# Moving one layer's table building behind the gate on the vector engine, in a one-core hybrid S5 / gated DeltaNet backbone

## The reference

```python
def swiglu(h, w13, w2):
    a, b = jnp.split(h @ w13, 2, axis=-1)
    return (jax.nn.silu(a) * b) @ w2
x = x + 0.5 * gate * swiglu(ada_norm(x, g, shift, scale), w13, w2)
...
abar = exp(dt * (a_re + i a_im))          # S5: 64 groups of 16 channels, 64 complex states each
h_t = abar * h_{t-1} + f * (B u_t)        # as an associative scan, in both directions
y_t = Re(C h_t)
```

## Time and profile before

| what | value |
|---|---|
| time, median of 3 runs | 2175.92 us (2172.47 to 2176.16) |
| profiled execution's own time | 2172.47 us |
| its span, first to last instruction | 2170.7 us |
| mean granted TensorE clock | 0.948 |
| PE / DVE / ACT / POOL busy | 1984.7 / 1476.4 / 698.9 / 589.1 us |

### The profile page before, as it was taken

How to read it: one execution, slowest core, us unless ns; L and a number is a source line. 1 busy time by engine, 2 the same in 40 slices (tenths; PEclk the granted TensorE clock), 3 DMA queues, 4 the chain that set the end, 5 groups by cost and what they waited for, 6 DMA issues and landing times.

```text
span 2170.7 us, 37461 instructions
## 1 busy us (share of the span) xinstructions
PE 1984.7 (91%) x14700; PEld 1684.0 (78%) x14700; DVE 1476.4 (68%) x2265; ACT 698.9 (32%) x1110; POOL 589.1 (27%) x473
## 2 busy tenths in 40 slices
PE   3999999991889899999979999998999999989997
PEld 0778778771788678888858888886888889879997
DVE  8958778764434596784889668346677777746555
ACT  2322222222123322221234222123555555426332
POOL 2254774752442231120233112023000000022113
PEclk9999999995759899999999999999999999889999
DMA  8364565549952354444535444222211111114553
GB/s 318 141 239 166 204 212 184 200 161 205 293 159 97 116 187 162 154 169 141 187 103 184 156 154 171 95 80 80 74 41 41 41 50 50 41 59 139 184 181 97
DMA packets 104736, 310.20 MB, mean 143 GB/s; under 512 B 27680, under 2 KB 39456, under 8 KB 95136
## 3 DMA queue, kind: packets, MB, share of 16 engines
q1 hardware_dynamic: 89392, 285.67, 39.6%
q10 hardware_dynamic: 12528, 12.33, 1.8%
q0 software_dynamic: 2688, 10.42, 1.2%
HBM read 280.13 MB, written 28.25 MB: 142 GB/s over the span
## 4 chain that ended last, share of the span: by engine, by line
PE 81%; DVE 8%; DMA 3%; ACT 2%; issue 2%; SPq 2%; POOL 2%; DVEq 0%; ACTq 0%; POOLq 0%
PE PS L229 40%; PE PS L1555 6%; PE PS L220 6%; PE PS L1542 6%; PE PS L222 6%; PE PS L221 6%; PE PS L1188 2%; DVE wlo L261 1%; DMA vwS<-vwd 1%; PE PS L609 1%; PE PS L1179 1%; DVE rstd L376 1%; PE PS L1059 1%; DVE junk L638 1%; PE PS L1161 1%
## 5 line engine op out<-in xcount | busy, mean ns | idle before, releaser
L261 DVE TENSOR_TENSOR wlo<-raw,whi 128x1024 fp32r<-128x1024 f32 x314 | 478.9, 1565 | 83.8 <-ACT whi L255 82.0
L229 PE MATMUL PS<-hh,whi 128*128 128x512 f32 (+1 forms) x1536 | 443.8, 371 | 39.4 <-DVE hl L397 29.1
L229 PE MATMUL PS<-hl,whi 128*128 128x512 f32 (+1 forms) x1536 | 439.8, 368 | 0.0
L229 PE MATMUL PS<-hh,wlo 128*128 128x512 f32 (+1 forms) x1536 | 438.6, 367 | 0.0
L255 ACT ACTIVATE whi<-raw 128x1024 fp32r<-128x1024 f32 x300 | 301.3, 1052 | 287.5 <-PE PS L222 253.6
L229 PEld LDWEIGHTS PS<-hh,whi 128*128 128x128 f32 x1536 | 278.4, 191 | 95.1 <-issue 45.8
L229 PEld LDWEIGHTS PS<-hl,whi 128*128 128x128 f32 x1536 | 280.7, 191 | 47.5
L229 PEld LDWEIGHTS PS<-hh,wlo 128*128 128x128 f32 x1536 | 279.7, 190 | 47.2
L590 POOL CAST hidh<-gt 128x512 f32 (+2 forms) x88 | 61.5, 699 | 858.9 <-DVE gt L537 858.9
L220 PE MATMUL PS<-hidh,whi 128*128 128x512 f32 (+1 forms) x704 | 259.3, 368 | 16.1 <-POOL hidl L592 10.3
L221 PE MATMUL PS<-hidl,whi 128*128 128x512 f32 (+1 forms) x704 | 256.5, 364 | 0.0
(11 more groups left out here) (325 smaller groups left out, 2812.8 us busy)
## 6 DMA issues: line engine op xcount, KB each, us to landing
modw<-in_mod_w SPq DMA_DIRECT2D x72, 1024.0 KB, 5.0
raw<-in_w_gdn SPq DMA_DIRECT2D x32, 512.0 KB, 4.0
cxd<-cx POOLq DMA_DIRECT2D x16, 576.0 KB, 3.3
cxS<-cxd SPq DMA_DIRECT2D x8, 1152.0 KB, 5.9
raw<-in_w_f0p0a SPq DMA_DIRECT2D x16, 512.0 KB, 6.9
vwd<-vws ACTq DMA_DIRECT2D x16, 512.0 KB, 8.1
raw<-in_w_f0p1a SPq DMA_DIRECT2D x16, 512.0 KB, 7.3
raw<-in_w_glu SPq DMA_DIRECT2D x16, 512.0 KB, 4.7
```

The source lines that it names most:

```text
L229: ended = pe.matmul(dst, of[:, slot, c:c + P], moving, start=first and part_ == 0, stop=last and part_ == 2)
L261: dve.tensor_tensor(wlo[:, s, c], raw[:, s, c], whi[:, s, c].bitcast(F32), ALU.subtract)\
```

## The change

All table work on VectorE is done behind the gate (in "b" slots behind the second update); bx(b,1) moves from slot TABLE_AT+2 to TABLE_AT+1, and the two functions become one, in the order cf, bx, zs for rising b, then bz. In a slot TABLE_AT[b] this gives zs(b-1), bx(b,0), bz(b). SP's `load_bc(b)` moves one slot earlier. No instruction is added or removed.

```diff
@@ gate(i, s), in ffn_dve
                     if mods_where(f, p):
                         mods_dve(dve, g, 2 * i + s)
-                    if f == 0:
-                        tables_first_dve(dve, BASE[a] + 2 * i + s)
                     dve.wait_ge(sil_ready[s], pairs + i + 1)
...
@@ update(i, s), in ffn_dve
                     add_to_x(dve, layer, n_, 4 * i + 2 * s, c0, 4, None).then_inc(x_ready[0], 1)
-                    if f == 0:
-                        tables_first_dve(dve, BASE[b] + 2 * i + s)
                     dve.wait_ge(blk_done[s], 1 + BASE[b] // 2 + i + 1)
...
@@ tables_sp
             for b in range(2, NB5):
-                if j == TABLE_AT[b]:
+                if j == TABLE_AT[b] - 1:
                     load_bc(sp, b)
...
-        def tables_first_dve(dve, j):
+        def tables_dve(dve, j):
...
             if j == 3:
                 dve.sem_inc(et_ready, 1)
             for b in range(NB5):
-                for r in range(2):
-                    if j == TABLE_AT[b] + 2 * r:
-                        bx_dve(dve, b, r)
-
-        def tables_dve(dve, j):
-
-            def step(ins):
-                step_dve(dve, ins)
-
-            for b in range(NB5):
                 if j == TABLE_AT[b] - 1:
                     cf_dve(dve, b)
+                for r in range(2):
+                    if j == TABLE_AT[b] + r:
+                        bx_dve(dve, b, r)
                 if j == TABLE_AT[b] + 3:
                     zs_dve(dve, b)
```

## The result

The changed kernel takes 2212.55 us (median of 4 runs, 2210.38 to 2216.3), the kernel before 2176.04 beside it: 1.0167 times as long, 95% interval 1.0144 to 1.019, or about +36.5 us. I had forecast 2192 and a range up to 2202. The direction is right, the size is off by a factor of two.

A forecast was written before the change was run, and what follows sets the result against it. The prediction took TensorE's pace to bound the first FFN; its terms, waits for late VectorE work plus low clock, summed to 17.6 us, giving 2190.1 or 2193.5 by baseline, forecast 2192 us, range 2176 to 2202.

The forecast's parts named there:

- slot 2, wait: Third weight block of the first FFN: TensorE waits for a split delayed by the et table behind gate(0), 2.1 us.
- slot 8, wait less that of before: bx(0,0) behind gate(6) makes TensorE wait 2.3 us, but today's 2.54 us hidl wait is almost used up: -0.2 net.
- slot 9, wait: bx(0,1) behind gate(7) delays VectorE's update that frees TensorE's accumulator: 1.6 us.
- slot 11, wait: bx(1,0) ahead of bz and split_lo(11) delays the update: 3.4 us, 0 uncontended, 5.2 if bz and both halves are contended.
- slots 12 to 19, 24 to 29: "a" blocks of the first FFN: VectorE stays just inside TensorE's slot, 0, up to 0.7 us in each of five places.
- slot 21, wait: Gate(19) late by bx(4,0), then bx(4,1) and the split delay the update TensorE wants: 3.1 us, 0 uncontended.
- slot 23, wait: Second group of "b" blocks: repeats the cost of slot 11, 3.4 us.
- slot 30, wait less that of before: Today's 1.40 us hidl wait gives way to the gate waiting for a contended split_lo(30): 0, from -1.4 to +0.8.
- low clock, net: Behind three new waits above 3 us TensorE's clock falls, 1.4 us each: 4.2, from 0 to 7.
- load moved: SP's load_bc one block earlier: 0; without cover 0.8 us for each of six blocks.
- heavier: Rival, chance 0.09: every third "a" slot waits, bz and splits all contended, low clock after each wait: about +28, 2203.

The follow-up runs named there:

- e4: Kernel before, with only SP's load of a batch's parameters moved one slot earlier: 2177.02 us against 2175.88, ratio 1.0004.
- e5: Changed kernel with GpSimd's six products of each cx replaced by two memsets: 2175.95 us, one run, against 2173.49 for the kernel before.
- e6: Kernel before with GpSimd's six products of each cx replaced by two memsets: 2181.23 us, one run, against 2173.49 for the kernel before.
- e10_bx_both_behind: Kernel before with both bx calls behind the gate, et tables and load not moved: 2206.75 us, one run, against 2174.47.
- e9_half_cx_later: Kernel before with bx(7,1) behind gate(29) and three of cx(0,0)'s six products moved to slot 7 behind hidl: 2171.07 us against 2174.47, ratio 0.9987.
- e2_bx1_behind: Kernel before with only bx(b,1) moved from before gate(8+3b) to behind gate(7+3b): 2177.53 us against 2175.88, ratio 1.0005.
- e1_et_behind: Kernel before with only the et tables of slots 0 to 3 moved behind the gate: 2178.83 us against 2175.88, ratio 1.001.
- e8_bx0_between: Changed kernel with bx(b,0) of slots 9 and 21 put back between the two updates: 2192.91 us, one run, against 2173.49 for the kernel before.

## Why the prediction was right in direction and wrong in size

By its own steps, changed kernel, in us:

| step | forecast | measured |
|---|---|---|
| slot 2, wait | 2.1 | 2.04 |
| slot 8, wait less that of before | -0.2 | -0.84 (1.70 - 2.54) |
| slot 9, wait | 1.6 | 3.40 |
| slot 11, wait | 3.4 (up to 5.2) | 5.96 |
| slots 12 to 19, 24 to 29 | 0 | 0 |
| slot 21, wait | 3.1 | 3.36 |
| slot 23, wait | 3.4 | 7.21 |
| slot 30, wait less that of before | 0 | +1.5 |
| low clock, net | 4.2 | 11.8 |
| load moved | 0 | within the noise (+1.0 in e4) |
| TensorE's slot 0, and what is not assigned | 0 | -0.7 and +0.8 |
| sum to the normalisation behind the FFN | 17.6 | 34.55 |

**Right.** Which slots wait and for what; that the gates of the "a" slots stay just inside their margin (TensorE is busy 108.20 of 108.20 us between 219.8 and 328); that GpSimd's cx beside the moved products is the cause (e5, e6); that the move of the load does nothing; and that gates made earlier give back little beside it (0.84 us and the low clock, in slot 8). In slot 0 the table ended at 79.34 instead of my 80.2, partly because TensorE's first slot was itself 0.7 us shorter, so the wait came out as forecast by two small errors.

**Wrong: the term of the clock.** The step that failed says "I give the three new waits above 3 us 1.4 each, 4.2". It took one row, the stretch behind a wait of 2.54 us, as the price, and counted three waits. Six waits of the changed kernel were followed by a fall, not three, and at 1.5 to 3.0 us each: the low stretch behind a wait lasted 3.0 to 6.3 us. This is 7.6 of the 17 missing, in this one profile: with waits only 1.9 us shorter, e10_bx_both_behind lost 7.5 to the clock in place of 13.6.

**Wrong: the waits of slots 9, 11, 23 and 30.** They measured 1.8, 2.6, 3.8 and 1.5 us more than the sum had, 9.7 together; slots 2, 8 and 21 give 0.4 back. For slot 11 the sum let bz and one half of the split run beside a quiet GpSimd, which costs 3.4; both halves and bz were contended, as in the upper bound of 5.2 that I gave and did not take. Since the bx products start and end beside cx(b,0), the split lands on cx(b,1), which follows it in a "b" slot with no gate between. The same holds in slot 23, where bz took 2.89 us and the split 4.50. In these two a step that starts later behind contended work meets the next contended work. Slot 9 failed on TensorE's side. VectorE's update ended at 172.88, where the sum has 172.8 (by luck: a small step behind the split, 1.16 us beside cx, was left out, and bx took 8.4 instead of 9.45). TensorE was ready at 169.62 in place of 171.2: its slot 0 was 0.7 shorter, slot 8 waited less than allowed, and the first stretch of slot 8 was taken as slow as before when its clock did not fall (1.00 in the window above). In slot 30 GpSimd was the late one. Gate(29) starts 0.95 us behind the end of TensorE's slot, no later than before (1.22), but GpSimd is busy with cx(7,1) and the issue of its transfer until 478.09, so hidh starts 3.49 us behind TensorE's slot instead of 1.98:

```profile
474.63 2.31 POOL L989 TENSOR_TENSOR cx<-cx,t 128x576 f32<-128x576 f32 x1
475.55 0.68 DVE L535 TENSOR_TENSOR gt<-gt,PS 128x512 f32<-128x512 f32 x1
478.09 0.62 POOL L586 CAST hidh<-gt 128x512 fp32r<-128x512 f32 x1
```

**The rival "heavier".** It named a low clock behind each wait and contended bz and splits, and was given 0.09 and +28; its third part, waits of the "a" slots, did not come. The range ended at 2202 because it was laid on this rival's smallness, not on the bounds of the terms: taking slots 11 and 23 at 5.2 and the clock behind seven waits at the 7 us that the prediction allowed for three would have given about +33.

## What to carry to other kernels

A VectorE product with both operands in SBUF took 0.69 us beside an idle GpSimd and 1.5 to 1.8 beside GpSimd's products here, so a list of VectorE work has to be placed by what GpSimd does at that moment, not only by VectorE's own slack; work that waits for nothing belongs into the stretch where GpSimd itself is waiting. When a TensorE-bound stage gets a new wait, count more than the wait: the matmuls behind it may run at the lower clock, which no list of waits shows. In these twelve profiles that added from nothing (e9_half_cx_later) to 1.2 times the waits' sum (e2_bx1_behind), and half of it in the changed kernel. And when several uncertain steps follow one another on one engine, take their upper bounds together, since a late start is what makes the next step contended.

## What was not expected of the hardware

The low clock behind a wait is not in proportion to it. In the changed kernel waits of 2.04, 2.94, 3.36, 3.40, 5.96 and 7.21 us were followed by 3.34, 6.22, 6.25, 2.98, 4.21 and (at 0.60) 5.79 us of about half clock, while a wait of 1.70 us was followed by none; in e1_et_behind a wait of 1.84 us brought 7.0 us at 0.53, and in e10_bx_both_behind and e8_bx0_between a wait of 2.92 us in slot 30 brought none. What decides it these runs don't show. The Trainium skill (SBUF — State Buffer, "Who interferes with whom") says that two-operand VectorE products contend with GpSimd's reads and not with its writes: light cx, which only writes, left bx at 0.69 us, and so agrees. Here is one such pair, from e5_after_light_cx:

```profile
184.81 1.23 POOL L987 MEMSET cx<- 128x576 f32 x2
184.95 0.69 DVE L940 TENSOR_TENSOR bx<-sB,pw 128x512 f32<-128x512 f32 x1
```
